# A gated recurrence in a one-core kernel: tile steps laid over the half-levels of the next round, and another order for the last three tiles

## The chip, the core and the metric

The kernel runs on one core of one Trainium2 chip. The metric is device time in microseconds; three runs of the kernel before gave 2991.47, 2984.78 and 2988.79 us, median 2988.79. TensorE (PE) multiplies matrices and transposes, VectorE (DVE), ScalarE (ACT) and GpSimd (POOL) work elementwise, and SyncE (SP) issues most DMAs. Each engine runs its instructions in the order in which they are written, and semaphores hold one until work elsewhere is done.

## The reference

Two layers of a streaming encoder over 1024 prompt tokens and 32 sample tokens. The change is in one part of layer 0, a gated recurrence with 4 heads of 128x128 state:

```
def _hgrn2_chunk(S0, xs):
    """Exact chunkwise form of S_t = diag(f_t) S_{t-1} + k_t v_t^T, o_t = S_t^T q_t."""
    ...
    att = jnp.einsum('bthk,btshk,bshk->bhts', q, decay, k)
    o = (jnp.einsum('bhts,bshv->bthv', att, v)
         + jnp.einsum('bthk,bhkv->bthv', q * jnp.exp(G), S0))
    S = (jnp.exp(G_end)[..., None] * S0
         + jnp.einsum('bshk,bshv->bhkv', k * jnp.exp(G_end[:, None] - G), v))
...
    ob = ob * lax.rsqrt(jnp.mean(ob * ob, axis=-1, keepdims=True) + EPS)
    ob = ob.reshape(B, T, B_VW) * g_norm.astype(F32) * jax.nn.silu(gb.astype(F32))
```

## The kernel before

The program is a row of phases with a barrier between any two: front, attention A, recurrence, trunk 0, attention C, trunk 1. The recurrence takes about 120 of 2989 us.

It works on tiles of 128 tokens: 0 to 7 are the prompt, tile 8 is the 32 sample tokens (padded) with a state of its own. Three rounds of three tiles each build the decayed products of a tile. A round goes through seven levels; a level has two half-levels, one for each pair of heads, so there are 14 steps, which the code counts as `at`. In a half-level, PE's `pairs` multiplies k by r into a bank of the ring (24 small matmuls, or 12 or 6 larger ones in slots 6 and 7), then DVE's `rise` scales r, DVE's `choose_pairs` keeps the masked part of the bank in `near`, and POOL scales k. `join` (DVE) makes the products of the next level. `pairs` of slot s+1 waits for `rise`, for POOL's product and for the mask of slot s-1. I write pairs(n,s,p) for round n, slot s, pair p. After the last slot ACT's `place` copies the results into the matrix `att`; in the last round `place_late` on DVE copies the near part.

While round n goes through its levels, the three tiles of round n-1 are carried through eight steps of their own, woven into the 14 (before, 16) values of `at` by `tiles_at(n - 1, at, offset)`. Tile j of the round has a step at `at = offset + 4 j`:

- `turn_keys` (PE, transpose of k) and `turned_keys` (ACT, copy to `kT`)
- `updates` (PE, kT by v into `dS`)
- `values` (PE, att by v plus r by the state, into the bank `out`; 8 matmuls)
- `state_update` (DVE, needs `updates` and `values`)
- `squares` (ACT, sums of squares and a square root), `inverse_roots` (DVE), `scaled` (ACT, `out` to `o`)
- `turn_out` (PE, transpose of o), `finish` (DVE, product with the gate)

`values` of a tile waits for `state_update` of the tile before, and, since there is one bank `out`, for its `scaled`. The gate (2112 KB) is loaded by SP late in round 0; ACT turns it by Silu and then scales it per head (`gate_scale`) in round 1. The last three tiles (in the order 6, 8, 7; positions 6, 7, 8) have no round above them. They are written out one after the other at the end, where position 7 uses free banks of the ring and the other two share the main ones. The last `finish` releases the store of the last columns and the barrier to trunk 0.

Of the kernel before, what the change touches and what calls it, by code (L numbers as in the profile page):

```python
# [24 lines left out]
P = 128  # L25
# [10 lines left out]
HB = 4  # L36
# [3213 lines left out]
def recurrence(nc, io, c, head, mix, next_weights, samples_stored, tiles_stored, tail_stored):  # L3250
# [11 lines left out]
    LAST = 2 * LEVELS + 2  # L3262
    with Tools(nc) as m:
# [11 lines left out]
        eps = m.sb("hg_eps", [P, 1])  # L3275
        ring = [[m.ps(f"hg_ring{b}{pr}", [P, 512]) for pr in range(2)] for b in range(2)]
# [50 lines left out]
        def bank(name, p):  # L3327

            main, spare = {"kT": (kT_ps, ring[0][0]), "out": (out, ring[0][1]), "dS": (dS, ring[1][0]), "turn": (turn, ring[1][1])}[name]
            return spare if p == SWAPPED else main  # L3330

        def bank_free(eng, name, p):

            if p == SWAPPED:
                if name in ("kT", "out"):
                    eng.wait_ge(placed_mid, 4 * ROUNDS)
                else:
                    eng.wait_ge(placed_far, 2 * ROUNDS)
                eng.wait_ge(masked, masked_no(ROUNDS - 1, SMALL, 1))
                return  # L3340
            before = p - 1 if p < SWAPPED else p - 2
            if before < 0:
                return
            if name == "kT":
                eng.wait_ge(kT_copied, before + 1)
            elif name == "dS":
                eng.wait_ge(state_ready, HB * (before + 1))
            elif name == "out":
                eng.wait_ge(o_scaled, HB * (before + 1))
            else:  # L3350
                eng.wait_ge(finished, before + 1)
# [51 lines left out]
        def _(dve):  # L3403
# [54 lines left out]
            def place_late():  # L3458
                n = ROUNDS - 1
                dve.wait_ge(out_done, 3 * (n - 1))  # L3460
                dve.wait_ge(att_zero, 2)
                dve.wait_ge(masked, masked_no(n, SMALL, 1))
                for b in range(4):
                    own_rows = slice(32 * b, 32 * b + 32)
                    dve.tensor_copy(att[n % 2][own_rows, :, 32 * b:32 * b + 32], near[n % 2][own_rows]).then_inc(placed_late, 1)

            for n in range(ROUNDS):
                if n:
                    dve.wait_ge(f_done, HB * n)
                    dve.wait_ge(q_done, n)  # L3470
                if n == ROUNDS - 1:
                    dve.wait_ge(f_pad, 1)
                    dve.wait_ge(q_pad, 1)
                for pr in range(2):
                    heads = slice(2 * pr, 2 * pr + 2)
                    dve.tensor_tensor(part(r, n, pr), q[n][:, heads, :], f[n][:, heads, :], ALU.mult).then_inc(r_ready, 1)
                for at in range(LAST):
                    lv, pr = divmod(at, 2)
                    if lv < LEVELS:
                        if pr == 0:  # L3480
                            join(n, lv)
                        rise(n, lv, pr)
                        if lv <= SMALL:
                            choose_pairs(n, lv, pr)
                    for t in tiles_at(n - 1, at, 2):
                        state_update(t)
                    for t in tiles_at(n - 1, at, 4):
                        inverse_roots(t)
                    for t in tiles_at(n - 1, at, 7):
                        finish(t)  # L3490
# [4 lines left out]
            inverse_roots(TILES - 1)  # L3495
            finish(TILES - 2)
            state_update(TILES)
            inverse_roots(TILES)
            finish(TILES - 1)
# [3 lines left out]
        def _(act):  # L3503
# [34 lines left out]

            def gate_scale(hd):
                if hd == 0:  # L3540
                    act.wait_ge(own.gate_in, 16)
                    act.activation(gate[:], gate[:], ACT.Silu).then_inc(gate_silu, 1)
                    act.wait_ge(gate_silu, 1)
# [3 lines left out]
            act.wait_ge(eps_set, 1)  # L3547
# [50 lines left out]
            for n in range(ROUNDS):  # L3598
                for at in range(LAST):
                    for t in tiles_at(n - 1, at, 0):  # L3600
                        turned_keys(t)
# [6 lines left out]
                place(n)  # L3608
            turned_keys(TILES - 2)
            turned_keys(TILES - 1)  # L3610
            squares(TILES - 2)
            turned_keys(TILES)
            squares(TILES - 1)
            scaled(TILES - 2)
            squares(TILES)
            scaled(TILES - 1)
# [3 lines left out]
        def _(pe):  # L3620
# [61 lines left out]
            def values(p):  # L3682
# [7 lines left out]
                else:  # L3690
                    pe.wait_ge(placed_late, 4)
# [11 lines left out]
                for hd in range(HB):  # L3703
# [3 lines left out]
                last.then_inc(out_done, 1)  # L3707
# [7 lines left out]

            for n in range(ROUNDS):
                for pr in range(2):
                    pairs(n, 0, pr)
                for at in range(LAST):
                    lv, pr = divmod(at, 2)  # L3720
                    if lv < LEVELS:
                        pairs(n, lv + 1, pr)
                    for t in tiles_at(n - 1, at, 0):
                        turn_keys(t)
                    for t in tiles_at(n - 1, at, 1):
                        updates(t)
                        values(t)
# [5 lines left out]
            values(TILES - 2)  # L3733
            updates(TILES - 1)
            values(TILES - 1)
            turn_keys(TILES)
            updates(TILES)
            values(TILES)
# [184 lines left out]
```

## Time and profile before

| | us |
|---|---|
| median of three runs | 2988.79 |
| the profiled execution | 2991.18 |
| its span | 2989.3 |
| recurrence, first to last instruction | 728.9 to 847.1 |
| round 0 | 728.9 to 753.7 |
| round 1, with tiles 0 to 2 | 753.7 to 792.5 |
| round 2, with tiles 3 to 5 | 792.5 to 824.4 |
| last three tiles | 824.4 to 847.1 |

The bounds of rounds 1 and 2 are the starts of DVE's first product of the round (L3476), and the last stretch begins with `place_late` (L3465). PE is busy for 2854.5 us of the whole span (95%), but the recurrence is a stretch in which it waits. A timeline row gives the start, the length, the engine, the line and the operation; rows of one operation in a sequence are merged (x8), and the bracket tells what ended the idle time before. Each fp32 matmul shows as two records, so `pairs` of 24 matmuls is x48.

### The profile page before, as it was taken

Reading aid. Unit: us, or ns where it says so; the run is one execution under the profiler, and the core shown is the slowest. Engines: PE = TensorE matmul, PEld = TensorE weight load, DVE = VectorE, ACT = ScalarE, POOL = GpSimd, SP = SyncE. Lnnn points to the kernel's source line nnn. Section 1 sums busy time; section 2 is a strip of 40 time slices with the busy share of each in tenths; the row PEclk is TensorE's granted clock in tenths of the full one; section 3 lists DMA queues with packets and bytes.
Section 4 is the critical chain, followed back from the end, with each engine's and each line's share of the span. In section 5 each row is a group of like instructions: output and inputs, shape, how many; then the busy total and the mean of one; then the engine's idle time right before and its main releaser. Section 6 shows DMA issues by size and latency. Waiting matters only on the chain. (4 is left out here: it accounts for less than half of the span.)

```text
span 2989.3 us, 61068 instructions
## 1 busy us (share of the span) xinstructions
PE 2854.5 (95%) x24985; PEld 2653.3 (89%) x24985; DVE 1742.2 (58%) x3136; ACT 1006.3 (34%) x2102; POOL 1533.6 (51%) x1377
## 2 busy tenths in 40 slices
PE   6999999997789999999999999999999999999998
PEld 4859999765689999999999999956699999999998
DVE  6399999656646744434787500066648543446785
ACT  3351111355433433333232311156525333333232
POOL 2121224464523777776577232144424777776675
PEclk8999999998889999999999999999999999999999
DMA  6716763652341122124222223163121212224321
GB/s 220 246 69 227 252 222 122 175 180 64 103 170 57 51 86 86 65 86 145 86 86 86 77 91 114 43 219 113 65 90 51 84 68 87 78 74 137 123 69 69
DMA packets 192053, 338.85 MB, mean 113 GB/s; under 512 B 27784, under 2 KB 107424, under 8 KB 189920
## 3 DMA queue, kind: packets, MB, share of 16 engines
q1 hardware_dynamic: 138832, 266.50, 26.7%
q10 hardware_dynamic: 52944, 68.45, 6.6%
q8 instruction: 199, 3.26, 0.4%
q14 instruction: 78, 0.64, 0.1%
HBM read 268.30 MB, written 79.49 MB: 116 GB/s over the span
## 5 line engine op out<-in xcount | busy, mean ns | idle before, releaser
L109 PE MATMUL tr_acc<-tr_quad_hi,ah_ring_hi 128*128 128x264 f32 x2432 | 694.1, 285 | 7.7 <-ACT tr_kept L1160 2.5
L740 POOL TENSOR_TENSOR ah_ring_lo<-ah_raw,ah_ring_hi 128x512 fp32r<-128x512 f32 (+2 forms) x426 | 578.9, 1366 | 237.6 <-ACT ah_ring_hi L1149 147.0
L111 PE MATMUL tr_acc<-tr_quad_hi,ah_ring_lo 128*128 128x264 f32 x2432 | 692.7, 285 | 0.0
L110 PE MATMUL tr_acc<-tr_quad_lo,ah_ring_hi 128*128 128x264 f32 x2432 | 690.3, 284 | 0.0
L109 PEld LDWEIGHTS tr_acc<-tr_quad_hi,ah_ring_hi 128*128 128x128 f32 x2432 | 458.7, 189 | 9.4 <-ACT tr_kept L1160 3.0
L110 PEld LDWEIGHTS tr_acc<-tr_quad_lo,ah_ring_hi 128*128 128x128 f32 x2432 | 458.7, 189 | 0.1
L111 PEld LDWEIGHTS tr_acc<-tr_quad_hi,ah_ring_lo 128*128 128x128 f32 x2432 | 458.2, 188 | 0.0
L2917 DVE CUSTOM_DVE_ANT_0 pc_prob<-pc_dots,pc_bias 128x640 f32<-128x640 f32 (+4 forms) x128 | 79.0, 655 | 283.1 <-POOL pc_bias L2720 261.7
L1779 DVE TENSOR_SCALAR_CACHE_REDUCE f_q<-score,choose_trial 128x384 bf16<-128x384 f32 (+6 forms) x224 | 242.2, 1145 | 1.1
L2083 POOL CAST f_w_hi<-f_raw 128x512 fp32r<-128x512 f32 x66 | 46.7, 708 | 375.9 <-DMA f_raw<-in_w_dram 204.8
L738 POOL CAST ah_ring_hi<-ah_raw 128x512 fp32r<-128x512 f32 (+1 forms) x114 | 72.6, 637 | 283.7 <-PE tr_acc L111 263.0
L109 PE MATMUL f_acc<-h_hi,f_w_hi 128*128 128x352 f32 x600 | 202.3, 337 | 8.7 <-DVE h_lo L2383 8.7
L1149 ACT ACTIVATE ah_ring_hi<-ah_raw 128x512 fp32r<-128x512 f32 x240 | 148.4, 624 | 165.8 <-POOL ah_raw L753 131.7
L109 PE MATMUL tr_acc<-tr_eighth_hi,ah_ring_hi 128*128 128x264 f32 x672 | 192.3, 286 | 4.5 <-DVE x L1567 3.4
L111 PE MATMUL f_acc<-h_hi,f_w_lo 128*128 128x352 f32 x600 | 193.6, 323 | 0.0
L110 PE MATMUL f_acc<-h_lo,f_w_hi 128*128 128x352 f32 x600 | 193.4, 322 | 0.0
L111 PE MATMUL tr_acc<-tr_eighth_hi,ah_ring_lo 128*128 128x264 f32 x672 | 191.3, 285 | 0.0
L110 PE MATMUL tr_acc<-tr_eighth_lo,ah_ring_hi 128*128 128x264 f32 x672 | 191.3, 285 | 0.0
L109 PE MATMUL tr_acc<-tr_mix_hi,ah_ring_hi 128*128 128x264 f32 x512 | 148.8, 291 | 7.2 <-DVE tr_mix_lo L1644 7.2
L109 PE MATMUL tr_acc<-tr_part_hi,ah_ring_hi 128*128 128x352 f32 x462 | 149.6, 324 | 0.0
L111 PE MATMUL tr_acc<-tr_part_hi,ah_ring_lo 128*128 128x352 f32 x462 | 148.7, 322 | 0.0
L110 PE MATMUL tr_acc<-tr_part_lo,ah_ring_hi 128*128 128x352 f32 x462 | 148.6, 322 | 0.0
(410 smaller groups left out, 7448.4 us busy)
## 6 DMA issues: line engine op xcount, KB each, us to landing
f_ada_w<-in_w_ada_dram SPq DMA_DIRECT2D x48, 1024.0 KB, 5.7
scratch_inner<-tr_kept ACTq DMA_DIRECT2D x88, 264.0 KB, 2.3
ah_raw<-in_w_gate_dram SPq DMA_DIRECT2D x44, 512.0 KB, 3.5
ah_raw<-in_w_up_dram SPq DMA_DIRECT2D x44, 512.0 KB, 4.5
ah_raw<-in_w_down_dram SPq DMA_DIRECT2D x64, 256.0 KB, 3.0
f_raw<-in_w_dram SPq DMA_DIRECT2D x24, 512.0 KB, 7.9
out_z_dram<-f_stage ACTq DMA_DIRECT2D x60, 176.0 KB, 2.0
out_z_dram<-tr_value ACTq DMA_DIRECT2D x48, 176.0 KB, 1.9
```

The lines of the kernel that those rows point to most:

```text
L109: pe.matmul(out, w_hi, hi, start=start, stop=False, skip_group_check=onto)
L110: pe.matmul(out, w_hi, lo, start=False, stop=False, skip_group_check=onto)
L111: return pe.matmul(out, w_lo, hi, start=False, stop=stop, skip_group_check=onto)
L738: pool.tensor_copy(hi[:, 0:width], own).then_inc(w_hi, 1)
L740: pool.tensor_tensor(lo[:, 0:width], own, hi[:, 0:width].bitcast(F32), ALU.subtract).then_inc(w_ready, 1)
L1149: act.activation(slot(u, to)[0], factor_of(u, to), ACT.Copy).then_inc(act_hi, 1)
L1779: last = dve.tensor_scalar(marks[n % 2][0:p, 0:width], score[0:p, at:at + width], bound(p, j), 0.0, compare, ALU.add, accum_out=count[0:p, ...
L2083: pool.tensor_copy(w[b].hi[:, own], raw[b][:, own]).then_inc(w_piece, 1)
L2917: dve.tensor_tensor_reduce(prob_of(s, hd)[:, 0:n], dots[hd][:, at_dots(s):at_dots(s) + n], add, -DH ** -0.5, 3.0e38, ALU.add, ALU.min, lea ...
```

## The change

1. DVE's steps of a tile move one `at` later (`state_update` 2 to 3, `inverse_roots` 4 to 5), `finish` moves from 7 to 6, and a round has 15 values of `at` instead of 16.
2. On PE, `turn_keys` and `updates` move one `at` earlier; the first tile's `turn_keys` stands ahead of the round's first `pairs`. `values` is cut in two calls of two heads each, at 1 and 2.
3. On ACT, the Silu of the whole gate and a first square root of one column (which loads its table) move from the middle of tile 0's steps to directly behind `place(0)`, ahead of tile 0's `turned_keys`.
4. At the end, PE runs the updates of positions 6 and 7 ahead of the values of 6, and the values of position 8 ahead of its updates. Position 8's values get the bank `ring[0][0]`, so they no longer wait for `scaled` of position 6. `place_late` makes eight copies instead of four: the four that the first tile needs, then four for the others. ACT and DVE have the last steps in another order.

```diff
-    LAST = 2 * LEVELS + 2
+    LAST = 2 * LEVELS + 1
@@ bank, bank_free
+            if name == "out" and p == TILES:
+                return ring[0][0]
...
+            if name == "out" and p == TILES:
+                eng.wait_ge(kT_copied, SWAPPED + 1)
+                return
@@ place_late
-                for b in range(4):
-                    own_rows = slice(32 * b, 32 * b + 32)
-                    dve.tensor_copy(att[n % 2][own_rows, :, 32 * b:32 * b + 32], near[n % 2][own_rows]).then_inc(placed_late, 1)
+                for tiles in (slice(0, 1), slice(1, 3)):
+                    for b in range(4):
+                        own_rows = slice(32 * b, 32 * b + 32)
+                        dve.tensor_copy(att[n % 2][own_rows, :, 32 * b:32 * b + 32].rearrange("p (h j) m -> p h j m", j=3)[:, :, tiles],
+                                        near[n % 2][own_rows].rearrange("p (h j) m -> p h j m", j=3)[:, :, tiles]).then_inc(placed_late, 1)
@@ vector
-                    for t in tiles_at(n - 1, at, 2):
+                    for t in tiles_at(n - 1, at, 3):
                         state_update(t)
-                    for t in tiles_at(n - 1, at, 4):
+                    for t in tiles_at(n - 1, at, 5):
                         inverse_roots(t)
-                    for t in tiles_at(n - 1, at, 7):
+                    for t in tiles_at(n - 1, at, 6):
                         finish(t)
...
+            state_update(TILES)
             finish(TILES - 2)
-            state_update(TILES)
+            finish(TILES - 1)
             inverse_roots(TILES)
-            finish(TILES - 1)
             finish(TILES)
@@ scalar
+            def gate_silus():
+                act.wait_ge(own.gate_in, 16)
+                act.activation(gate[:], gate[:], ACT.Silu).then_inc(gate_silu, 1)
+                act.wait_ge(eps_set, 1)
+                act.activation(root_first[:], eps[:], ACT.Sqrt)
...
-                    for t in tiles_at(n - 1, at, 0):
-                        turned_keys(t)
+                    if at >= 3:
+                        for t in tiles_at(n - 1, at, -1):
+                            turned_keys(t)
...
                 place(n)
+                if n == 0:
+                    gate_silus()
+                if n + 1 < ROUNDS:
+                    turned_keys(3 * n)
...
+            scaled(TILES - 2)
             squares(TILES - 1)
-            scaled(TILES - 2)
+            scaled(TILES - 1)
             squares(TILES)
-            scaled(TILES - 1)
             scaled(TILES)
@@ tensor
+                if n:
+                    turn_keys(3 * (n - 1))
                 for pr in range(2):
                     pairs(n, 0, pr)
...
+                    if at >= 3:
+                        for t in tiles_at(n - 1, at, -1):
+                            turn_keys(t)
                     for t in tiles_at(n - 1, at, 0):
-                        turn_keys(t)
+                        updates(t)
                     for t in tiles_at(n - 1, at, 1):
-                        updates(t)
-                        values(t)
+                        values(t, first_heads)
+                    for t in tiles_at(n - 1, at, 2):
+                        values(t, last_heads)
...
             updates(TILES - 2)
-            values(TILES - 2)
             updates(TILES - 1)
-            values(TILES - 1)
+            values(TILES - 2, range(HB))
             turn_keys(TILES)
+            values(TILES - 1, range(HB))
+            values(TILES, range(HB))
             updates(TILES)
-            values(TILES)
```

PE at the start of round 1, before (`hg_ring` is `pairs`, `hg_kT_ps` `turn_keys`, `hg_dS_ps` `updates`, `hg_out_ps` `values`):

```order
L3646 MATMUL hg_ring00<-hg_q1,hg_k 32x32 x24
L3646 MATMUL hg_ring01<-hg_q1,hg_k 32x32 x24
L3646 MATMUL hg_ring10<-hg_r,hg_k 32x32 x24
L3665 MATMUL hg_kT_ps<-ident,hg_k 128x128 x4
L3646 MATMUL hg_ring11<-hg_r,hg_k 32x32 x24
L3678 MATMUL hg_dS_ps<-hg_v,hg_kT0 128x128 x4
L3705 MATMUL hg_out_ps<-hg_v,hg_att0 128x128
L3706 MATMUL hg_out_ps<-hg_state0,hg_r 128x128
```

The same place after the change:

```order
L3680 MATMUL hg_kT_ps<-ident,hg_k 128x128 x4
L3661 MATMUL hg_ring00<-hg_q1,hg_k 32x32 x24
L3661 MATMUL hg_ring01<-hg_q1,hg_k 32x32 x24
L3661 MATMUL hg_ring10<-hg_r,hg_k 32x32 x24
L3693 MATMUL hg_dS_ps<-hg_v,hg_kT0 128x128 x4
L3661 MATMUL hg_ring11<-hg_r,hg_k 32x32 x24
L3720 MATMUL hg_out_ps<-hg_v,hg_att0 128x128
L3721 MATMUL hg_out_ps<-hg_state0,hg_r 128x128
L3720 MATMUL hg_out_ps<-hg_v,hg_att0 128x128
L3721 MATMUL hg_out_ps<-hg_state0,hg_r 128x128
L3661 MATMUL hg_ring00<-hg_r,hg_k 32x32 x24
```

The transposes now lead the round, `updates` stands ahead of pairs(1,1,1), and a `pairs` lies between the halves of `values`.

ACT from the end of `place(0)` to tile 0's first square, before (`hg_kT0<-hg_kT_ps` is `turned_keys`, `hg_junk0` `squares`):

```order
L3571 ACTIVATE hg_att0<-hg_near0 32x12x32 x4
L3578 ACTIVATE hg_kT0<-hg_kT_ps 128x512
L3542 ACTIVATE hg_gate<-hg_gate 128x4224
L3544 ACTIVATE hg_gate<-hg_gate,hg_gnorm_6704 128x1056 x4
L3585 ACTIVATE hg_junk0,hg_rstd<-hg_out_ps 128x128 x4
```

The same place after the change:

```order
L3581 ACTIVATE hg_att0<-hg_near0 32x12x32 x4
L3549 ACTIVATE hg_gate<-hg_gate 128x4224
L3551 ACT_TABLE_LOAD
L3551 ACTIVATE hg_root_first<-hg_eps 128x1
L3588 ACTIVATE hg_kT0<-hg_kT_ps 128x512
L3555 ACTIVATE hg_gate<-hg_gate,hg_gnorm_6704 128x1056 x3
L3588 ACTIVATE hg_kT1<-hg_kT_ps 128x512
L3555 ACTIVATE hg_gate<-hg_gate,hg_gnorm_6704 128x1056
L3595 ACTIVATE hg_junk0,hg_rstd<-hg_out_ps 128x128 x4
```

The Silu and a table load now stand ahead of the first copy of turned keys.

PE in the last stretch, before, from the transposes of positions 6 and 7:

```order
L3665 MATMUL hg_kT_ps<-ident,hg_k 128x128 x4
L3665 MATMUL hg_ring00<-ident,hg_k 128x128 x4
L3678 MATMUL hg_dS_ps<-hg_v,hg_kT0 128x128 x4
L3705 MATMUL hg_out_ps<-hg_v,hg_att0 128x128
L3706 MATMUL hg_out_ps<-hg_state0,hg_r 128x128
```

The same place after the change:

```order
L3680 MATMUL hg_kT_ps<-ident,hg_k 128x128 x4
L3680 MATMUL hg_ring00<-ident,hg_k 128x128 x4
L3693 MATMUL hg_dS_ps<-hg_v,hg_kT0 128x128 x4
L3693 MATMUL hg_ring10<-hg_v,hg_kT1 128x128 x4
L3720 MATMUL hg_out_ps<-hg_v,hg_att0 128x128
L3721 MATMUL hg_out_ps<-hg_state0,hg_r 128x128
```

The updates of position 7 (`hg_ring10`) have moved ahead of the eight matmuls of position 6's values.

## Rows read from the trace of the kernel before

**Rows 1.** Windows by stretch: length, busy us and count per engine, granted clock, DMA share

```profile
753.70:792.50 38.80, 27.80 (x796) 24.17 (x799) 23.61 (x55) 22.24 (x58) 21.03 (x19) 0.84 0.24 83
792.50:824.40 31.90, 24.63 (x712) 21.52 (x700) 22.86 (x54) 13.08 (x52) 17.15 (x16) 0.92 0.27 94
824.40:847.10 22.70, 16.83 (x92) 14.92 (x92) 8.78 (x23) 9.74 (x44) 9.92 (x11) 0.73 0.35 106
```

**Rows 2.** Timeline of SP, the DMA issues around the gate: start, length, operation

```profile
748.38 1.14 SPq L3243 DMA_DIRECT2D hg_gate<-out_z_dram  x1
759.28 0.37 SPq L3245 DMA_DIRECT2D hg_v<-out_zt_dram  x1
```

**Rows 3.** Timeline of ACT, start of round 1

```profile
760.08 0.60 ACT L3578 ACTIVATE hg_kT<-hg_kT_ps 128x512 f32<-128x512 f32 x1 [4.37 <-PE hg_kT_ps L3665]
760.71 3.73 ACT L3542 ACTIVATE hg_gate<-hg_gate 128x4224 f32<-128x4224 f32 x1
769.88 1.28 ACT L3588 ACT_TABLE_LOAD   x1
```

**Rows 4.** Timeline of PE, round 1 and the start of round 2

```profile
760.77 2.08 PE L3678 MATMUL hg_dS_ps<-hg_v,hg_kT 128*128 128x128 f32 x8
...
772.00 1.16 PE L3678 MATMUL hg_dS_ps<-hg_v,hg_kT 128*128 128x128 f32 x8 [2.60 <-ACT hg_kT L3578]
...
776.43 0.78 PE L3646 MATMUL hg_ring<-hg_r,hg_k 128*32 128x32 f32 x48
...
796.56 0.39 PE L3705 MATMUL hg_out_ps<-hg_v,hg_att 128*128 128x128 f32 x2
...
798.44 0.40 PE L3646 MATMUL hg_ring<-hg_r,hg_k 128*32 128x32 f32 x24
799.96 0.85 PE L3646 MATMUL hg_ring<-hg_r,hg_k 128*32 128x32 f32 x72 [1.13 <-issue]
```

**Rows 5.** Windows: the clock after PE's waits, columns as in rows 1

```profile
772.00:776.40 4.40, 4.40 (x24) 4.08 (x24) 0.55 (x3) 0.98 (x4) 0.00 (x0) 0.67 0.00 0
825.70:831.60 5.90, 5.58 (x24) 5.32 (x25) 2.12 (x3) 0.45 (x1) 5.64 (x7) 0.50 0.95 295
```

**Rows 6.** Timeline of DVE and ACT between two tiles of round 2

```profile
810.45 1.12 DVE L3439 SCALAR_TENSOR_TENSOR hg_state<-hg_state,hg_prod,hg_dS_ps 128x128 f32<-128x128 f32 x4
813.63 0.36 DVE L3418 COPY_PREDICATED hg_near<-hg_masks,hg_ring 128x192 f32<-128x192 int32 x1
813.89 0.16 DVE L3448 RECIPROCAL hg_rstd<-hg_rstd 128x4 f32<-128x4 f32 x1
814.09 1.14 ACT L3595 ACTIVATE hg_o<-hg_out_ps,hg_rstd 128x128 f32<-128x128 f32 x4 [1.18 <-DVE hg_rstd L3448]
```

**Rows 7.** Timeline of PE, one tile's distance in round 2

```profile
806.70 0.64 PE L3705 MATMUL hg_out_ps<-hg_v,hg_att 128*128 128x128 f32 x2
...
811.06 0.63 PE L3646 MATMUL hg_ring<-hg_r,hg_k 128*32 128x32 f32 x48 [0.24 <-POOL hg_k L3397]
811.62 0.66 PE L3665 MATMUL hg_kT_ps<-ident,hg_k 128*128 128x128 f32 x4
...
815.37 0.46 PE L3705 MATMUL hg_out_ps<-hg_v,hg_att 128*128 128x128 f32 x2 [0.55 <-ACT hg_o L3595]
```

**Rows 8.** Timeline of DVE, PE and ACT, the last stretch

```profile
824.44 3.44 DVE L3465 COPY hg_att<-hg_near 32x384 f32<-32x384 f32 x4
828.09 0.77 PE L3705 MATMUL hg_out_ps<-hg_v,hg_att 128*128 128x128 f32 x2 [0.30 <-issue]
838.05 0.46 PE L3705 MATMUL hg_out_ps<-hg_v,hg_att 128*128 128x128 f32 x2 [1.32 <-ACT hg_o L3595]
841.54 0.28 ACT L3585 ACTIVATE hg_junk<-hg_out_ps 128x128 f32<-128x128 f32 x1 [3.63 <-PE hg_out_ps L3706]
842.91 1.12 ACT L3595 ACTIVATE hg_o<-hg_ring,hg_rstd 128x128 f32<-128x128 f32 x4
846.37 0.69 DVE L3455 TENSOR_TENSOR hg_gate<-hg_turn_ps,hg_gate 128x512 f32<-128x512 f32 x1 [1.30 <-PE hg_turn_ps L3713]
```

More of the change, by code:

```diff
@@ L3275, in recurrence @@
         eps = m.sb("hg_eps", [P, 1])
+        root_first = m.sb("hg_root_first", [P, 1])
         ring = [[m.ps(f"hg_ring{b}{pr}", [P, 512]) for pr in range(2)] for b in range(2)]
@@ L3537, in _ @@
                 silus(n)
+            def gate_silus():
[3 more added lines that the diff above has]
+                act.activation(root_first[:], eps[:], ACT.Sqrt)
             def gate_scale(hd):
[L3540 to L3543, printed above, removed]
+                act.wait_ge(gate_silu, 1)
                 act.activation(gate[:, hd, :], gate[:, hd, :], ACT.Copy, scale=head.gnorm[:, hd:hd + 1]).then_inc(gate_done, 1)
             act.wait_ge(att_zero, 2)
-            act.wait_ge(eps_set, 1)
             def place(n):
@@ L3680, in updates, with values @@
                 last.then_inc(dS_done, 1)
-            def values(p):
+            def values(p, heads):
                 t = tile_at[p]
@@ L3690, in values @@
                 else:
-                    pe.wait_ge(placed_late, 4)
+                    pe.wait_ge(placed_late, 4 if j == 0 else 8)
                 for pr in range(2):
@@ L3702, in values @@
                 bank_free(pe, "out", p)
-                for hd in range(HB):
+                for hd in heads:
                     own_out = bank("out", p)[:, P * hd:P * hd + P]
@@ L3706, in values @@
                     last = pe.matmul(own_out, r[:, hd, P * t:P * t + P], state[s][:, hd, :], start=False, stop=True)
-                last.then_inc(out_done, 1)
+                if heads[-1] == HB - 1:
+                    last.then_inc(out_done, 1)
             def turn_out(p):
@@ L3714, in turn_out @@
                 last.then_inc(o_turned, 1)
+            first_heads, last_heads = range(HB // 2), range(HB // 2, HB)
             for n in range(ROUNDS):
+                if n:
+                    turn_keys(3 * (n - 1))
                 for pr in range(2):
```

## The prediction

> **What bounds the kernel now.** I read the page first: PE is busy for 95% of the span, so time can only be won where it waits. The windows by stretch [rows 1] show one such place, the recurrence: in round 1 PE is busy for 27.80 of 38.80 us, in round 2 for 24.63 of 31.90, in the last stretch for 16.83 of 22.70, the last with a mean granted clock of 0.73. No phase works beside the recurrence, and a barrier follows it, so a microsecond won or lost there should be one at the end, if trunk 0 starts from the same state. The whole question is how long rounds 1 and 2 and the last stretch take.
>
> The timelines then show what a tile costs. In round 2, values of tile 4 begin at 806.70 and of tile 5 at 815.37, a distance of 8.67 us [rows 7]. It is set by a ring: values wait for `scaled` of the tile before, that for `inverse_roots`, and that for its turn in DVE's row behind rise and choose, which wait for PE's pairs [rows 6, 7]. Two places are worse. In round 1 PE waits 2.60 us for ACT's second copy of keys, since ACT was with the gate (3.73 us of Silu, then the scales) and loading the root's table (1.28) [rows 3, 4], and the clock goes to a mean of 0.67 right behind it [rows 5]. In the last stretch all of values and updates from 825.70 to 831.60 run at 0.50 [rows 5], and position 8's values wait for `scaled` of position 6 [rows 8].
>
> **Start of round 1.** The Silu of the gate now stands ahead of tile 0's key copy. The gate's DMA is issued at 748.38, and SP's next issue, which waits for its landing, is at 759.28 [rows 2]. ACT is done with `place(0)` at 760.08 - 4.37 = 755.71 [rows 3], so it now waits 3.6 us for the gate, where before it copied keys and came to the gate when it had landed. From there: 759.3 + 3.73 Silu + 1.28 table = 764.3, 0.2 for a root of one column, and the copy of 0.60 [rows 3] ends at 765.1. Before it ended at 760.68. PE meets this wait earlier than before, since `updates` of tile 0 now stand ahead of pairs(1,1,1), and queued behind them are pairs(1,1,1), the values and the next levels, on which DVE and POOL wait. That is a new wait of about 6 us (pairs(1,1,0) are through at about 759). Updates at the lower clock take 2.08 us [rows 4], then pairs 0.87 and half the values 1.75 (all eight took 1.88 at the full clock, 796.56 to 798.44 [rows 4]; I take double for four at the low one). I carry it on: tile 0's values start at 768.1; pairs(1,2,0), the other half, pairs(1,2,1), the transposes, pairs(1,3,0), updates and pairs(1,3,1) bring PE to about 775.6; DVE, which has 1.12 us of `state_update` and the join in front, is through rise, choose and root at 776.9; `scaled` ends at 778.2, values of tile 1 start at 778.35 and pairs(1,4,0) at 779.3. Before they started at 776.43 [rows 4]. So the Silu's own former stall (2.60) is gone, and what comes in its place is 2.9 us later.
>
> **One tile in the new order.** PE's pieces at the full clock: pairs 0.60, transposes 0.60 (811.06 to 811.62 and 0.66 [rows 7]), updates 1.0, half the values 0.94. Between two starts of values stand 4 pairs, both halves, turn_out, turn_keys and updates: 2.4 + 1.9 + 1.2 + 1.0 = 6.5 us. The last piece ahead of the next values is now pairs(·,·,1), and only behind it come rise 0.47, choose 0.26, root 0.20, `scaled` 1.14 and 0.14 to PE's start (813.63, 813.89, 814.09 and 815.37 [rows 6, 7]): 2.25 us in which PE has nothing, since the halves of values stand first in its row. Sum 8.75 where before it was 8.67: the work that lay beside this chain (updates, 1.0) has moved ahead of it, and DVE's inverse has moved from behind rise(·,0) to behind rise(·,1). Where DVE or POOL is late it is more: for the first tile of a round I get 9.2 from DVE's row (state 1.12, join and two rises), for the others 9.1, between 8.75 and 9.6 by whether POOL's product or DVE's rise goes first.
>
> **Round ends.** Behind the third tile's values come 10.0 us to DVE's first product of the next round: 4.6 to 5.4 to pairs(·,7,1), then state 1.12, join, two rises, root, `scaled` 1.14, turn_out and finish (9.6 to 10.4 in all). Before it was 824.44 - 815.37 = 9.1 [rows 7, 8]: one `at` less in the table, but state and inverse now stand later. So round 1 ends at 778.35 + 9.1 + 10.0 = 797.4, against 792.5 [rows 1]: **+4.9** (+3.5 to +6).
>
> **Round 2.** Its first key copy is again behind `place`, and now in PE's way: I get 5.0 to the first values, then 9.2 + 9.1 + 10.0 = 33.3 us. Before: 31.9 [rows 1], with 1.13 of "issue" inside [rows 4], which I leave out of mine. **+1.3** (-0.5 to +2.4).
>
> **The last stretch.** Before, from `place_late` (824.44) to the end of the last finish (847.06) 22.6 us [rows 8]; the values start 3.65 in. Now both updates stand ahead, so the four early copies (some 2 us of the 3.44) are hidden: updates of 6 start at 1.5, and at the low clock seen there before (2.08 each) the values of 6 at 5.5, ended at 8.0 as the clock comes back. From there ACT is the chain: squares with root 1.37 (841.54 to 842.91), the last key copy 0.6, then scaled, squares, scaled, squares, scaled (1.14 and 1.37 each [rows 8], with 0.2 to 0.6 for DVE's roots), 8.9 in all, then turn_out and finish 1.4: 18.3. The wait for the bank is gone, and the last values run beside ACT. **-4.3**; with the full clock throughout -7.1, with the low one for longer and copies held up by POOL -2.5.
>
> Sum: 4.9 + 1.3 - 4.3 = +1.9 us. On the profiled execution 2991.18 + 1.9 = 2993.1; that execution stood 2.4 above the median of the runs, and from the median it is 2988.79 + 1.9 = **2990.7 us**. About 0.2% (6 us) is what can be told from no change here.
>
> **A page's price for the table load.** The row shows 1.28 us of load and the next instruction at once behind it [rows 3]. The Trainium skill, ScalarE: Activation LUTs, What ACT_TABLE_LOAD costs, says that a drain of about 1.38 us comes with each switch, 2.66 in all. By it the key copy that now stands behind the load would be another 1.4 us later, and the sum +3.3. The sum above goes by the row.
>
> **Rivals.** (1) Slower: the low clock at each tile. Each tile but the rounds' first now has a bare wait of 2.25 us in front of its values, near the 2.60 behind which the clock fell to a mean of 0.67 [rows 4, 5]; before, such waits were mostly filled by updates. If it falls each time, values, one pairs and a transpose cost about 1.7 more, at tiles 1, 2, 4 and 5: +6.8, and 2997.5. It decides once two or three of the four fall. For it: the 2.60. Against it: shorter waits of 0.55 and 1.42 passed at the full clock, and round 2 had a mean of 0.92 [rows 1]. (2) Faster: everything comes at its ideal. The clock is back as soon as PE works again in round 1 (-1.5), the tiles keep 8.15 to 8.75, round 2 comes out at -0.5 and the last stretch at -7.1: 3.4 - 1.5 - 0.5 - 7.1 = -5.7, and with the 1.13 of issue won as well -6.8, so 2982. For it: PE has less mixed work in the last stretch, and steadier work could hold the clock. Against it: all must hold at once, and the gate's landing at 759.28 is not touched. (3) The change doesn't do what it says: the new wait at the gate falls away, because the gate lands earlier. Then round 1 wins instead: key copy at 761.5, values of tile 1 at about 772, -3.5 to -6, and in sum about 2981. SP's issues ahead of the gate are unchanged, so I give it little.
>
> **Chances.** Forecast 0.48, its own range 2986 to 2995; rival 1 0.30; rival 2 0.15; rival 3 0.04; the rest of 0.03 is even. A part of the forecast's cases lies beyond +6 (0.03), and a part of rival 2 within 6 (0.03). So faster 0.18, same 0.49, slower 0.33. The range takes in rival 1's middle and stops just above rival 2's: 2983 to 2998.
>
> **What would show it.** ACT's Silu starts behind an idle of about 3.6 us that a DMA ended, and PE waits about 6 us for the first key copy. PE then shows a bare wait of 2.2 us for ACT's `scaled` ahead of each later tile's first half of values, and starts of values stand 8.7 to 9.6 us apart. Rounds 1 and 2 take about 43.7 and 33.3 us, the last stretch 18.3. The clock in the windows behind the bare waits tells rival 1. I am wrong if values come under 8 us apart, if the Silu finds the gate landed, or if trunk 0 takes back or adds what the recurrence gave.

## The result: slower by 10.4 us, and the profile after

Six runs of the changed kernel gave 2997.31 to 3001.07 us, median 2998.51, against 2988.12 (2983.05 to 2991.47) for six of the kernel before: ratio 1.004, 95% interval 1.003 to 1.005. I had forecast 2990.7 with a range of 2983 to 2998. The direction was a rival's (slower, 0.33), the size just outside the range.

The profiled execution took 2997.31 us. Its stretches, as in [rows 1] (length, busy us and count per engine, granted clock, DMA share):

```profile
748.40:794.30 45.90, 27.07 (x748) 23.70 (x748) 25.60 (x54) 22.33 (x60) 22.31 (x19) 0.80 0.20 67
794.30:834.60 40.30, 27.80 (x746) 24.53 (x745) 23.25 (x54) 13.41 (x53) 20.81 (x19) 0.84 0.22 75
834.60:852.00 17.40, 11.97 (x94) 10.65 (x92) 12.88 (x27) 9.48 (x43) 7.33 (x8) 0.97 0.46 137
```

Round 1 took 45.9 us (before 38.8), round 2 40.3 (31.9), the last stretch 17.3 (22.6), round 0 24.8 (24.7): +10.2 in the recurrence. My terms were +4.9, +1.3 and -4.3; measured +7.1, +8.3 and -5.3. These two executions differ by only 6.1 us in all (2997.31 against 2991.18), because the phases ahead of the recurrence, which the change does not touch, happened to take 5.3 us less in the changed kernel's profile (the recurrence starts at 723.62 and not at 728.92). So one pair of profiles doesn't account for the +10.4 of the medians. More profiles do, in the table below: without round 0 the recurrence took a mean of 92.2 us in three profiles of the kernel before and 102.7 in two of the changed one, +10.4.

The start of round 1 came as forecast. ACT, in timeline rows as in [rows 3], and the copy that PE waits for:

```profile
753.75 3.72 ACT L3549 ACTIVATE hg_gate<-hg_gate 128x4224 f32<-128x4224 f32 x1 [3.30 <-DMA hg_gate<-out_z_dram]
757.50 1.28 ACT L3551 ACT_TABLE_LOAD   x1
758.79 0.20 ACT L3551 ACTIVATE hg_root_first<-hg_eps 128x1 f32<-128x1 f32 x1
758.90 0.58 ACT L3588 ACTIVATE hg_kT<-hg_kT_ps 128x512 f32<-128x512 f32 x1
```
```profile
759.53 2.07 PE L3693 MATMUL hg_dS_ps<-hg_v,hg_kT 128*128 128x128 f32 x8 [5.79 <-ACT hg_kT L3588]
```

The Silu stands behind an idle of 3.30 us that the gate's DMA ended (I had 3.6), PE waits 5.79 us (6). The copy is through 35.9 us behind the kernel's first product at 723.62, forecast 765.1 - 728.9 = 36.2; values of tile 1 start 24.2 us into the round, forecast 24.7. The root starts where the table load ends (757.50 + 1.28). The drain of about 1.4 us that the Trainium skill (ScalarE: Activation LUTs, What ACT_TABLE_LOAD costs) adds is not in this trace.

What failed is the distance from there on. PE between the values of tiles 1 and 2, to be set against [rows 7]:

```profile
772.61 0.46 PE L3720 MATMUL hg_out_ps<-hg_v,hg_att 128*128 128x128 f32 x2 [2.27 <-ACT hg_o L3605]
...
778.57 1.13 PE L3693 MATMUL hg_dS_ps<-hg_v,hg_kT 128*128 128x128 f32 x8 [0.93 <-DVE hg_state L3445]
779.63 0.63 PE L3661 MATMUL hg_ring<-hg_r,hg_k 128*32 128x32 f32 x48
...
782.53 0.46 PE L3720 MATMUL hg_out_ps<-hg_v,hg_att 128*128 128x128 f32 x2 [2.27 <-ACT hg_o L3605]
```

The bare wait of 2.27 us ahead of the values is the 2.25 I had worked out. The 0.93 us ahead of the updates, released by DVE's state, I had not. Distance 9.92 us, where I had 9.1 and the kernel before 8.67. That 8.67 was itself disturbed: its first two matmuls of values took 0.64 us instead of 0.46 [rows 7], the lower clock. Five other profiles with the old rounds (e11, e1, e8, e15, e17, below) give 8.27 to 8.29 for the same distance, so the change costs about 1.6 us for each tile at the full clock. DVE and ACT inside that wait, as in [rows 6]:

```profile
780.30 0.56 DVE L3415 TENSOR_TENSOR hg_r<-hg_r,hg_prod 128x384 f32<-128x384 f32 x1 [0.81 <-PE hg_ring L3661]
780.77 0.37 DVE L3424 COPY_PREDICATED hg_near<-hg_masks,hg_ring 128x192 f32<-128x192 int32 x1
781.04 0.17 DVE L3454 RECIPROCAL hg_rstd<-hg_rstd 128x4 f32<-128x4 f32 x1
```
```profile
781.24 1.14 ACT L3605 ACTIVATE hg_o<-hg_out_ps,hg_rstd 128x128 f32<-128x128 f32 x4 [2.17 <-DVE hg_rstd L3454]
```

PE's last pairs start at 779.63 and are through at 780.26. Only then come rise, choose and the reciprocal, and PE stands idle under all of it.

The round's end, DVE, then POOL, then PE:

```profile
787.72 1.11 DVE L3445 SCALAR_TENSOR_TENSOR hg_state<-hg_state,hg_prod,hg_dS_ps 128x128 f32<-128x128 f32 x4
...
788.95 2.31 DVE L3415 TENSOR_TENSOR hg_r<-hg_r,hg_prod 128x384 f32<-128x384 f32 x2
791.18 0.17 DVE L3454 RECIPROCAL hg_rstd<-hg_rstd 128x4 f32<-128x4 f32 x1
```
```profile
788.92 0.83 POOL L3403 TENSOR_TENSOR hg_k<-hg_k,hg_prod 128x384 f32<-128x384 f32 x1 [0.70 <-PE hg_ring L3669]
789.72 2.23 POOL L3391 TENSOR_SCALAR hg_k<-hg_f 128x768 f32<-128x768 f32 x2
```
```profile
792.58 1.12 PE L3729 MATMUL hg_turn_ps<-ident,hg_o 128*128 128x128 f32 x4 [3.74 <-ACT hg_o L3605]
```

The last two rises take 2.31 us where two alone take about 1.1. POOL is at work on its next complement meanwhile (789.72, two in 2.23), and I read the second rise as held up by it. The reciprocal stands behind it, PE waits 3.74 us, and the round ends 11.8 us behind the start of its last values (I had 10.0; before 9.1 to 9.5).

The last stretch, to be set against [rows 8]:

```profile
834.63 7.77 DVE L3472 COPY hg_att<-hg_near 32x128 f32<-32x128 f32 x8
842.43 1.12 DVE L3445 SCALAR_TENSOR_TENSOR hg_state<-hg_state,hg_prod,hg_dS_ps 128x128 f32<-128x128 f32 x4
851.28 0.69 DVE L3461 TENSOR_TENSOR hg_gate<-hg_turn_ps,hg_gate 128x512 f32<-128x512 f32 x1 [1.92 <-PE hg_turn_ps L3729]
```
```profile
838.68 0.46 PE L3720 MATMUL hg_out_ps<-hg_v,hg_att 128*128 128x128 f32 x2 [1.01 <-issue]
842.61 0.46 PE L3720 MATMUL hg_ring<-hg_v,hg_att 128*128 128x128 f32 x2 [1.47 <-issue]
```

Eight small copies (four of 32x128, then four of 32x256; the merged row names the first form alone) took 7.77 us where four of 32x384 took 3.44 [rows 8], and the state of position 6 had to wait for them. PE's waits of 1.01 and 1.47 us are marked issue, but both end 0.2 us behind a copy (the fourth ends at 838.47, the eighth at 842.40), and `values` waits for four and for eight copies there. So the early copies were not hidden, as I had it. They ran beside POOL's preparation of weights for a later phase (`ah_ring`), so the recurrence doesn't have the chip to itself, as the prediction said. All the same the stretch came out 1.0 shorter than forecast: its granted clock was 0.97, and the values of position 6 started 4.05 us in, not 5.5.

Stretches of all profiles (us; the last column is the ratio to the kernel before by the times, with its interval):

| kernel | round 0 | round 1 | round 2 | last | 1, 2 and last | ratio |
|---|---|---|---|---|---|---|
| before | 24.7 | 38.8 | 32.0 | 22.6 | 93.4 | |
| before, e11 | 24.6 | 38.2 | 31.3 | 19.5 | 89.0 | |
| before, e14 | 26.5 | 38.8 | 34.9 | 20.6 | 94.4 | |
| changed | 24.8 | 45.9 | 40.3 | 17.3 | 103.6 | 1.004 (1.003 to 1.005) |
| changed, e12 | 29.4 | 43.8 | 40.7 | 17.3 | 101.8 | |
| e1 tail only | 26.7 | 38.8 | 33.9 | 16.5 | 89.2 | 0.9994 (0.9982 to 1.0005) |
| e2 rounds only | 25.4 | 48.7 | 37.0 | 23.3 | 109.0 | 1.0071 (1.0055 to 1.0086) |
| e3 updates late | 25.1 | 47.7 | 41.0 | 17.3 | 106.1 | 1.0039 (1.0025 to 1.0054) |
| e4 gate back | 24.8 | 45.0 | 43.5 | 17.3 | 105.9 | 1.0033 (1.0021 to 1.0044) |
| e5 DVE back | 30.9 | 37.8 | 31.5 | 16.6 | 85.9 | 1.0000 (0.9988 to 1.0013) |
| e6 DVE, gate back | 25.1 | 37.1 | 34.7 | 18.1 | 89.9 | 0.9998 (0.9988 to 1.0008) |
| e7 before, DVE moved | 26.9 | 43.1 | 37.5 | 20.0 | 100.6 | 1.0058 (1.0037 to 1.0078) |
| e8, e15, e17 tail, four copies | 30.5, 27.6, 24.5 | 39.9, 38.2, 38.2 | 31.3, 31.4, 31.6 | 15.8, 16.3, 15.7 | 87.0, 86.0, 85.5 | 0.9990 (0.9981 to 0.9999) |
| e9, e16, e18 | 30.9, 27.4, 26.5 | 36.4, 37.4, 37.4 | 33.3, 34.9, 35.7 | 15.5, 15.7, 16.9 | 85.1, 88.0, 90.0 | 0.9989 (0.9980 to 0.9998) |
| e10 inverse back | 28.8 | 40.8 | 33.4 | 16.9 | 91.1 | 1.0006 (0.9993 to 1.0019) |
| e13 before, inverse moved | 24.8 | 40.0 | 34.3 | 20.1 | 94.4 | 1.0024 (1.0011 to 1.0037) |

The ratios of the two groups of three are those of e17 and e18.

### The profile page after: what moved, and what is told of

Same layout as the page of the kernel before. It is cut to its first block and busy times, and to the rows that moved or that the text cites. A ratio compares the mean times of both kernels' runs of the same rounds, so it can differ in the third digit from the quotient of the medians.

```text
span 2995.4 us, 61091 instructions
## 1 busy us (share of the span) xinstructions
PE 2846.7 (95%) x24985; PEld 2646.6 (88%) x24985; DVE 1751.7 (58%) x3140; ACT 1006.9 (34%) x2103; POOL 1536.6 (51%) x1377
## 3 DMA queue, kind: packets, MB, share of 16 engines
q1 hardware_dynamic: 138832, 266.50, 26.7%
```

## The experiments

**Which half: e1 and e2.** e1 has before's rounds and the changed last stretch, e2 the reverse.

> Rounds 0 to 2 as before, only the last stretch as changed (order, bank of its own, eight copies). In the changed kernel the last stretch took 17.3 us, before 22.6. Theory A (the parts are independent): the last stretch is 17.3 again, total 5.3 below before, about 2982.8. Theory B (the stretch was good only because PE came to it at another level of the clock): 20 us, total 2.6 below before.

> Rounds as changed, the last stretch as before (four copies, old order, one bank). Theory A: rounds 1 and 2 take 45.9 and 40.3 us as in the changed kernel, the last stretch 22.6, total 15.4 above before, about 3003.5. Theory B (the last stretch gives part of it back by itself): under 12 above before.

e1: 2989.40 us against 2989.07; e2: 3010.98. The loss is in the rounds. The last stretch is short in both kernels that have its new order (16.5, 17.3), but e1's time shows no gain, and e2 lost more than theory A allows: its rounds took 85.7 us, as in the changed kernel, and its last stretch as before. The times say 21.9 us above the kernel before, theory A 15.4. Its profiled execution (3003.61 us) was the fastest of its six, so what made the others longer isn't in a trace; that stays open.

**PE's part: e3.**

```diff
                     for t in tiles_at(n - 1, at, 1):
+                        updates(t)
                         values(t, first_heads)
```

(and no `updates` at 0.)

> The changed kernel with `updates` one half-level later, directly ahead of the first half of values, as before; all else changed. Theory A (updates stand in PE's chain and meet a wait for the state of the tile before, since there is one dS bank): the 0.93 us wait on DVE's state goes and the 1.0 us of updates fills the bare 2.27 us wait, so values of two tiles stand about 8.0 us apart and not 9.9, 1.9 less at four distances, total 7.6 below the changed kernel, about 2991. Theory B (DVE's row and its lock with POOL set the distance): 9.5 us apart, total at most 2 below the changed kernel.

3000.97 us, 2.5 above the changed kernel: theory A fell, and theory B's 9.5 us is not what came either. Its values of round 1:

```profile
774.81 0.46 PE L3720 MATMUL hg_out_ps<-hg_v,hg_att 128*128 128x128 f32 x2 [2.96 <-ACT hg_o L3605]
...
785.87 0.46 PE L3720 MATMUL hg_out_ps<-hg_v,hg_att 128*128 128x128 f32 x2 [2.61 <-ACT hg_o L3605]
```
```profile
771.15 1.26 DVE L3415 TENSOR_TENSOR hg_r<-hg_r,hg_prod 128x384 f32<-128x384 f32 x1
773.32 0.17 DVE L3454 RECIPROCAL hg_rstd<-hg_rstd 128x4 f32<-128x4 f32 x1
```

The wait for the dS bank is gone, and the bare wait has grown to 2.96 and 2.61 us. What PE waits for hangs on the reciprocal in DVE's row, behind two rises, of which the first took 1.26 us beside POOL's product against 0.56. Moving PE's own work gained nothing. How much worse e3's order is by itself can't be said: the distances were 10.2 to 12.0 us, but PE's granted clock behind all four bare waits was 0.53 to 0.69 (windows of 3.5 us), so the low clock is in them.

**The gate: e4.** The Silu back behind tile 0's key copy, the table load at the first root.

> The changed kernel with the gate's Silu back behind tile 0's key copy and the root's table load back at the first root; all else changed. Theory A (the wait for the gate's DMA costs what PE waits, 5.8 us): tile 0's values start about 5.5 us earlier; the Silu and scales then stand before the first squares, which costs 1 to 2 again, so round 1 is 4 to 5 us shorter and the total about 2994. Theory B (ACT only moves its stall to tile 1, and the round is set by what follows): under 1.5 us.

2998.32 us, ratio 1.0033: theory B. Tile 0's values did start 5.85 us earlier, but round 1 was only 0.9 shorter. Its trace, PE's start of tile 1's values and the windows around it:

```profile
767.37 0.77 PE L3719 MATMUL hg_out_ps<-hg_v,hg_att 128*128 128x128 f32 x2 [2.30 <-ACT hg_o L3606]
```
```profile
763.00:767.00 4.00, 2.07 (x54) 1.71 (x53) 2.62 (x6) 2.50 (x7) 1.76 (x2) 0.50 0.02 4
767.00:771.00 4.00, 3.63 (x60) 3.37 (x61) 0.71 (x2) 0.23 (x1) 0.60 (x1) 0.50 0.00 0
779.00:783.00 4.00, 3.33 (x35) 3.07 (x36) 0.56 (x2) 0.53 (x3) 0.45 (x1) 0.60 0.00 0
```

Values of tiles 1 and 2 ran at a clock of 0.50 and 0.60. For tile 1 the clock was low already ahead of its bare wait (0.50 from 763.00), behind an issue gap of 1.50; for tile 2 it was 1.00 up to the wait and low behind it. In round 2, two more waits of 2.27 us were followed by 0.50 and 0.62, and the mean over rounds 1 and 2 was 0.75 where the changed kernel had 0.82. That is nearly my rival 1: the low clock at all four tiles, at three of them from the bare wait on. So e4 doesn't tell what the wait for the gate costs by itself: the low clock may have taken back what the earlier start gained.

**DVE's part: e5, e6, e7.** `state_update`, `inverse_roots` and `finish` back to 2, 4 and 7 (e5), the gate back too (e6), and the kernel before with these three moved to 3, 5 and 6 (e7):

```diff
-                    for t in tiles_at(n - 1, at, 3):
+                    for t in tiles_at(n - 1, at, 2):
                         state_update(t)
-                    for t in tiles_at(n - 1, at, 5):
+                    for t in tiles_at(n - 1, at, 4):
                         inverse_roots(t)
-                    for t in tiles_at(n - 1, at, 6):
+                    for t in tiles_at(n - 1, at, 7):
                         finish(t)
```

> The changed kernel with only DVE's tile steps at their old places (state 2, inverse 4, finish 7, 16 values of `at`). Theory C (DVE's moves are what costs: the inverse behind rise(.,1) makes the bare 2.3 us wait, the state behind it the 0.93 us wait for the dS bank, and both stand in the chain at a round's end): values stand 7.6 to 8.5 us apart instead of 9.9, rounds end 8.6 to 9.5 behind the last values instead of 11.8, together 12 to 15 below the changed kernel, about 2985, at or under before. Theory D (the halves of values and the early updates on PE cost): distance stays over 9.3, total at most 4 below the changed kernel.

> As e5_dve_back, and the gate's Silu and the root's table back where they were. Theory C: PE's first wait of 5.8 us goes, ACT is late at tile 0's squares instead (as in e4), so 1 to 5 below e5, about 2982, faster than before. Theory D: as e4, 2994 or more.

> The kernel before with only DVE's tile steps moved as in the change (state 3, inverse 5, finish 6, 15 values of `at`). Theory C: a round ends 11.5 behind its last values instead of 9.1 to 9.5 and tiles stand 0.3 to 1 further apart: 6 to 9 above before, about 2996. Theory D: within 2 of before.

e5: 2989.23 us, ratio 1.0000, and rounds 1 and 2 take 69.3 us against 86.2; e7 (four runs): 3002.28 against 2988.15, ratio 1.0058. Theory C holds in its direction from both sides: DVE's numbers alone make the loss in the kernel before, and with them back PE's new order shows none. Its sizes were off: e5 isn't faster than the kernel before, and e7 lost 14 us, not 6 to 9. Tiles stand 8.37 apart in both rounds of e5 (second distance), and a round ends 9.0 to 9.5 behind its last values; in e7 it ends 11.9 and 12.6 behind. At that distance of 8.37 us PE still has a bare wait ahead of the values:

```profile
786.41 0.46 PE L3720 MATMUL hg_out_ps<-hg_v,hg_att 128*128 128x128 f32 x2 [1.50 <-ACT hg_o L3605]
```

The old rounds have 0.55 to 0.85 there and stand 8.28 apart. So the length of a bare wait alone doesn't tell the distance. e6 is no different from e5 in time (2986.17 us, intervals overlap), where theory C had it faster than before. In e5 the wait for the gate had shrunk to

```profile
765.95 2.07 PE L3693 MATMUL hg_dS_ps<-hg_v,hg_kT 128*128 128x128 f32 x8 [0.79 <-ACT hg_kT L3588]
```

because its round 0 was 6.1 us longer: the gate's transfer runs beside round 0, so a slow round 0 hides it. `finish` and `state_update` were never moved alone.

**Which of the three: e10 and e13.** Only `inverse_roots` back to 4 in the changed kernel (e10), only `inverse_roots` at 5 in the kernel before (e13).

> The changed kernel with only `inverse_roots` back at 4 (state 3, finish 6, 15 values of `at` as changed). Theory G (the inverse is half of the cost: it makes the bare wait at each tile and stands behind the held-up rise(6,1) at a round's end): 0.7 less at four distances, 1.6 less at two ends, about 6 below the changed kernel, 2992. Theory H (the later state is the whole cost): at most 2 below the changed kernel.

> The kernel before with one number changed: `inverse_roots` at 5 instead of 4. Theory G (the inverse behind rise(.,1) puts `scaled` behind PE's last pairs): a bare wait at each tile, though updates (1.0) fill part of it, 0.3 to 1 at four distances, and at two round ends 1.6 for rise(6,1) that POOL's complement holds up: 4 to 7 above before. Rival K (the cost needs the earlier updates and the later state): at most 2 above before.

e10: 2989.44 us, ratio 1.0006 where the changed kernel has 1.0040. One number takes back about 10 us, each kernel set against the runs of before made beside it, more than theory G's 6. The granted clock isn't what changed: its mean over rounds 1 and 2 is 0.82 in both kernels' profiles. Its PE, values of tiles 1 and 2 and the round's end:

```profile
773.00 1.13 PE L3693 MATMUL hg_dS_ps<-hg_v,hg_kT 128*128 128x128 f32 x8 [0.67 <-DVE hg_state L3445]
...
776.14 0.46 PE L3720 MATMUL hg_out_ps<-hg_v,hg_att 128*128 128x128 f32 x2 [1.45 <-ACT hg_o L3605]
...
784.41 0.46 PE L3720 MATMUL hg_out_ps<-hg_v,hg_att 128*128 128x128 f32 x2 [0.62 <-ACT hg_o L3605]
...
793.37 1.12 PE L3729 MATMUL hg_turn_ps<-ident,hg_o 128*128 128x128 f32 x4 [2.64 <-ACT hg_o L3605]
```

The bare waits are 1.45 and 0.62 instead of 2.27, the wait at the end 2.64 instead of 3.74; second distances are 8.27 in both rounds, at the full clock, as in the old rounds. Between tiles 1 and 2 the distance fell from 9.92 to 8.27 and the bare wait from 2.27 to 0.62, both by 1.65, while the wait for the dS bank ahead of tile 2's updates stayed at 0.93 (the 0.67 is tile 1's). So with the inverse early the wait for the bank costs nothing. A round ends 10.7 us behind its last values, in e5 9.0 to 9.5; what is left there belongs to the later state or the earlier `finish`, which e10 keeps.

e13: 2995.17 us against 2988.49, ratio 1.0024 (1.0011 to 1.0037): +7 by the medians, theory G's upper end, and rival K doesn't hold. PE of e13:

```profile
808.71 0.46 PE L3705 MATMUL hg_out_ps<-hg_v,hg_att 128*128 128x128 f32 x2 [1.99 <-ACT hg_o L3595]
...
818.13 0.46 PE L3705 MATMUL hg_out_ps<-hg_v,hg_att 128*128 128x128 f32 x2 [2.06 <-ACT hg_o L3595]
```

Waits of 1.99 and 2.06 us ahead of the values, in a kernel whose PE order is the old one with updates right ahead of them; before it was 0.55 [rows 7]. The second distance of round 2 is 9.42 us against 8.28, so 1.14 of the 1.65 us comes with the late inverse alone. The round ends did not grow: 9.56 and 9.57 us (before 9.1 to 9.5), where theory G had 1.6 each; the last two rises took 1.04 us together there, so no rise was held up. Rounds 1 and 2 took 74.3 us in its one profile against 69.5 to 73.7 before, a mean of 71.3, so the trace shows about 3 of the 7 us, and where the rest lies stays open. e7, with the state and finish moved as well, is another 10 us above e13, and its profile shows the most of it at the round ends (11.9 and 12.6 against 9.6): late state and late inverse together make them long.

**Copies: e8.** e1 with four copies of all three tiles instead of eight.

> As e1_tail_only, but with the four copies of before instead of eight; all else of the last stretch as changed. Each small copy took about 0.97 us beside POOL's casts, whatever its size (eight: 7.8 us, four before: 3.4). Theory E (a copy waits for one POOL instruction, so their number counts and not their size): the copies take 3.4 to 3.9, the state of position 6 no longer waits for them, and the last stretch is about 1 shorter, 15.5 to 16.5. Theory F (the early four are what starts the values sooner): no shorter, or longer by up to 1.

2984.63 us, ratio 0.9991 (0.9978 to 1.0004); the last stretch 15.84 against 16.52 in one profile each (16.3 and 15.7 in e15 and e17), and the copies took 3.45, theory E:

```profile
829.25 3.45 DVE L3470 COPY hg_att<-hg_near 32x384 f32<-32x384 f32 x4
```

**More profiles, and the version with the useful parts: e9, e11, e12, e14 to e18.** e9 is the changed kernel with DVE's steps, the gate and the four copies as before.

> The changed kernel with DVE's tile steps, the gate's Silu, the root's table and the four copies of `place_late` back as before; what stays of the change is PE's order in the rounds, the halves of values and the order and bank of the last stretch. Theory C with E: rounds 1 and 2 about 69 to 72 us in sum (86.2 changed, 70.8 before), last stretch 15.8 to 16.5 (17.3, 22.6): 4 to 7 below before, about 2983. Rival: the spread of PE's issue gaps and of the clock hides it, within 2 of before.

> The kernel before, profiled once more. Round 0 is the same program in every kernel here and took 24.7 to 30.9 us, with PE gaps of 0.2 to 3.1 us that end in issue, always at the same matmuls. Theory I (the gaps are of the execution and not of the kernel): they differ here from the first profile of the same kernel by over 1 us in sum, and rounds 1 and 2 stay within 2 us of 70.8. Rival: the gaps are the kernel's own and come back as they were.

> The changed kernel, profiled once more. Distances of values in round 1 of 9.9 us with bare waits of 2.27 and 0.93, and 11.8 at the round's end, if the order sets them; they come back to 0.1 us. The low clock and the issue gaps may fall elsewhere: the stage without round 0 within 3 us of 103.6.

> The kernel before, a third profile. Theory I (gaps of issue fall anew in each execution): round 0 may take anything from 24.6 to 31. Theory L (they belong to the kernel): 24.6 to 24.8 a third time.

> The kernel of e8, profiled again: round 0 took 30.45. Theory I: another value, by over 2 us as likely as not. Theory L: 30.5 again, and that is where its last stretch's gain went. The last stretch 15.8 again.

> The kernel of e9, profiled again: round 0 took 30.85. Theory I: another value. Theory L: 30.9 again. The last stretch 15.5 again, rounds 1 and 2 within 2 of 69.6.

e9's time was 2985.53 against 2986.17, no difference, where theory C with E had 4 to 7 less. e12 gave the waits of the changed kernel's round 1 back to 0.03 us (2.27, 2.27, 0.90, 0.93 and 3.74), so they are the order's. Round 0, the same program in all, took 24.7, 24.6 and 26.5 in three profiles of before, 24.8 and 29.4 in two of the changed kernel, 30.5, 27.6 and 24.5 in three of e8's. By e11 alone theory I had missed (24.6 came back); e12, e15 and e16 decide for it: the gaps of PE's issue fall anew in each execution, and theory L is out. e16's rounds 1 and 2 took 72.3 us, 2.6 off e9's and beyond the 2 expected. A profile of one execution has some 5 us of luck in it.

The last question was whether the shorter last stretch shows in time:

> The kernel of e8 (rounds as before; last stretch in the new order with its own bank, four copies). Without round 0 the stage took 87.0 and 86.0 us, before 93.4, 89.0 and 94.4 (mean 92.2). Theory M (what the stage saves is saved): 4 to 6 below before, ratio about 0.998. Rival N (trunk 0 gives it back): ratio 0.9995 to 1.0005.

> The kernel of e9 (PE's order in the rounds, halves of values, new last stretch; DVE, gate and copies as before). Without round 0 85.1 and 88.0 us. Theory M: 4 to 7 below before, ratio about 0.998, same as e17 within 2 us. Rival N: ratio 0.9995 to 1.0005.

e17: 2984.56 and e18: 2984.13 us against 2986.55; 2.0 to 2.4 below, with intervals that just leave 1.000 out. The intervals of the same two kernels in e8 and e9 took it in (e9: 0.9997, 0.9986 to 1.0009), so a gain over the kernel before is likely and small. Neither theory as stated: less than the 4 to 6 of M. Both are well under the changed kernel. That PE's new order in the rounds (e18 against e17) adds anything isn't shown.

## Why the prediction was wrong, step by step

- **Start of round 1**: mechanism and size right (wait 5.79 against 6, values of tile 1 at 24.2 against 24.7). What it is worth stays open: with the wait taken out (e4, e6) no time was won that could be measured, but in e4 the low clock stood in the way, and in e5, which e6 is set against, in its profile a long round 0 had hidden most of the wait.
- **One tile in the new order**: the step that failed. I had seen that the inverse behind rise(.,1) makes a bare wait of 2.25 us, and then booked it as nearly even (8.75 to 9.2 against 8.67), because updates moved out of its way. Measured 9.92 at the full clock, 11.50 and 11.26 in round 2 with PE's issue gaps (1.25 and 0.55) and the low clock at tile 4. The old rounds at the full clock have 8.28, and with the inverse one step earlier the new ones have 8.27 (e10). So the late reciprocal made the loop from values to values longer, by 1.65 us at the second distance of a round and 0.9 at the first of round 1 (10.27 against 9.33), and the work that moved away paid for none of it. I also missed that `updates` of a tile need the dS bank which the state of the tile before reads, 0.93 us; e10 shows that this wait costs only together with the late inverse.
- **Round ends**: sized 10.0, measured 11.8 and 11.6. I had put two free rises ahead of the reciprocal, and they took 2.31 us instead of 1.1. With the inverse early the ends take 10.7 (e10), with all three of DVE's steps back 9.0 to 9.5 (e5), and with the inverse alone late in the old kernel 9.6 (e13). So it takes the later state, or the moved `finish`, as well; which of the two isn't shown.
- **Round 2**: +1.3 forecast, +8.3 measured in that execution. The first values came 5.9 us in (I had 5.0), the two distances were 4.5 over mine and the end 1.6. In these 7.0 us are 2.4 of issue gaps, of which I had allowed for none in my order while they stood in before's.
- **The last stretch**: -4.3 forecast, -5.3 measured against 22.6. But three profiles of before give 22.6, 19.5 and 20.6: the first was the slowest, with a granted clock of 0.73 where the others had 0.94 and 0.92. Against their mean of 20.9 the gain is 3.6. That the size came near is in part luck: the low clock I had in the sum did not come, and the copies I had hidden did cost.
- **The sum**: +10.1 measured against +1.9 in these stretches. The start of round 1 gave -0.4 of the difference, the three later distances +5.3, the two round ends +3.4, the start of round 2 +0.9 and the last stretch -1.0.
- **Rival 1** (low clock at each bare wait) gave 2997.5, near the result. It came near for another reason. In the changed kernel's profile the low clock came at one of four tiles:

```profile
770.30:772.60 2.30, 0.04 (x4) 0.02 (x1) 1.44 (x4) 1.14 (x4) 1.28 (x1) 1.00 0.00 0
772.60:776.40 3.80, 3.72 (x116) 3.34 (x116) 1.28 (x3) 0.00 (x0) 1.18 (x1) 1.00 0.02 4
809.50:811.80 2.30, 0.03 (x2) 0.06 (x1) 1.44 (x4) 1.14 (x4) 1.28 (x1) 1.00 0.00 0
811.80:815.80 4.00, 4.00 (x64) 3.71 (x65) 0.84 (x2) 0.00 (x0) 1.06 (x1) 0.57 0.02 4
```

Two waits of the same 2.27 us, PE's clock 1.00 behind the one and 0.57 behind the other. In e12 it was one of four again, in e2 two, in e3 and e4 all four, in e10 and e13 none. So it adds to the loss of the changed kernel, and doesn't carry it. Rival 2 did not come; rival 3 is excluded by ACT's wait of 3.30 us.

## What to carry to other kernels

When an instruction moves by one slot, find which engine's last work it now stands behind. A reciprocal of 0.17 us, moved by one step, cost about 7 us in the old kernel, and moved back in the changed one it returned about 10, because everything that PE needed next hung on it and it had moved behind the last product PE itself had to deliver. If an edit makes a loop through several engines longer, count that in full; other work that moves out of its way at the same time doesn't pay for it. Measure the loop by the distance from values to values and not by the wait alone: e5 had a bare wait of 1.50 us at a distance of 8.37, the old rounds 0.55 to 0.85 at 8.28. And take the base line of a short stretch from more than one execution.

## What the runs showed of the hardware

- DVE and POOL: copies of 32x128 and 32x256 beside POOL's casts took about as long as those of 32x384, 0.97 and 0.86 us each (7.77 for eight, 3.44 for four). In these two rows the number of DVE instructions set the time, and hardly their size.
- PE's gaps that end in issue stood at much the same places of round 0 (some 5, 10, 16 and 22 us in, not all of them each time) and were 0.2 to 3.4 us long, anew in each execution; they summed to 1.0 us in the shortest round 0 (24.5 us, e17) and to 7.9 in e8's and e9's (30.5 and 30.9). What makes them isn't shown.
